# A two-layer hybrid encoder on one core: ten of the first layer's 22 feed-forward blocks by seven products of quarter size, the second layer's state-space maps prepared in the other twelve blocks

## The reference, cut to what matters

```python
for l in range(2):                       # DEPTH
    ...                                  # attention branch, state-space branch, gates, W_o
    x = x + (gate_a * branch_a + gate_b * branch_b) @ w_o[l]
    x = x + _swiglu(_rmsnorm(x, norm2_g[l]), w_ffn_gate[l], w_ffn_up[l], w_ffn_down[l])

def _swiglu(x, w_gate, w_up, w_down):
    return (jax.nn.silu(x @ w_gate) * (x @ w_up)) @ w_down
```

## Time and profile before

| what | value |
|---|---|
| median of 3 runs | 1522.54 us (1522.38 to 1523.39) |
| the profiled execution's own time | 1524.58 us |
| span of its instructions | 1522.4 us |
| TensorE busy | 1486.8 us, 98% |
| VectorE busy | 1099.5 us, 72% |
| ScalarE busy | 670.6 us, 44% |
| GpSimd busy | 462.0 us, 30% |
| first layer's feed-forward, first product to last | 413.4 to 799.7 us |
| second layer's feed-forward begins | 1167.9 us |

### The profile page before, as it was taken

The page is one execution under the profiler, slowest core; times in us unless marked ns, Lnnn a source line. Parts: engine busy times, 40 slices in busy tenths (PEclk is TensorE's granted clock), DMA queues, the critical chain, the costliest instruction groups (busy, mean ns, idle before and its releaser), DMA issues.

```text
span 1522.4 us, 23041 instructions
## 1 busy us (share of the span) xinstructions
PE 1486.8 (98%) x8954; PEld 1221.0 (80%) x8954; DVE 1099.5 (72%) x1469; ACT 670.6 (44%) x1146; POOL 462.0 (30%) x254
## 2 busy tenths in 40 slices
PE   8999998999999999999999999999999999999998
PEld 3555897878878878887888888887787998998997
DVE  5999888768448997568432782586888995896794
ACT  4563258852452222232332413587435652453361
POOL 0000053544444454443544323444542120110010
PEclk9999999999999999999999999999999999999999
DMA  6568720142333244443437642102331333234223
GB/s 248 163 195 294 296 84 1 43 124 83 97 113 97 77 167 158 145 140 112 163 106 276 214 153 89 56 1 70 111 103 65 111 97 126 84 99 137 70 92 116
DMA packets 73499, 189.51 MB, mean 124 GB/s; under 512 B 23600, under 2 KB 32176, under 8 KB 69296
## 3 DMA queue, kind: packets, MB, share of 16 engines
q1 hardware_dynamic: 41952, 145.18, 28.3%
q10 hardware_dynamic: 31440, 42.87, 8.7%
HBM read 155.52 MB, written 32.51 MB: 124 GB/s over the span
## 4 chain that ended last, share of the span: by engine, by line
PE 67%; DVE 17%; DVEq 5%; ACT 4%; issue 3%; DMA 1%; POOLq 1%; POOL 1%; SPq 0%; ACTq 0%
PE ps L2146 20%; PE ps L2148 20%; PE ps L2147 20%; PE ps L2295 2%; DVE wl L1999 2%; DVE work L1382 1%; ACT prob L1148 1%; PE ps L2201 1%; PE ps L2272 1%; DVEq L1562 1%; DVEq L1509 1%; PE ps L2240 1%; DVE wsum L1990 1%; PE ps L2286 1%; PE ps L2459 1%
## 5 line engine op out<-in xcount | busy, mean ns | idle before, releaser
L632 POOL TENSOR_TENSOR wl<-stage,wh 128x1024 fp32r<-128x1024 f32 x138 | 356.7, 2591 | 645.2 <-ACT wh L730 456.2
L730 ACT ACTIVATE wh<-stage 128x1024 fp32r<-128x1024 f32 (+2 forms) x178 | 181.0, 1023 | 221.9 <-PE ps L2148 103.4
L2146 PE MATMUL ps<-XH,wh 128*128 128x256 f32 x616 | 174.8, 284 | 3.7 <-DVE wl L1999 2.8
L2148 PE MATMUL ps<-XH,wl 128*128 128x256 f32 x616 | 173.8, 282 | 0.0
L2147 PE MATMUL ps<-XLr,wh 128*128 128x256 f32 x528 | 148.5, 281 | 0.0
L2146 PE MATMUL ps<-xg2h,wh 128*128 128x512 f32 x352 | 140.3, 399 | 0.0
L2148 PE MATMUL ps<-xg2h,wl 128*128 128x512 f32 x352 | 139.2, 396 | 0.0
L2147 PE MATMUL ps<-xg2l,wh 128*128 128x512 f32 x352 | 139.2, 396 | 0.0
L2146 PEld LDWEIGHTS ps<-XH,wh 128*128 128x128 f32 x616 | 116.8, 190 | 5.2 <-DVE wl L1999 3.2
L2148 PEld LDWEIGHTS ps<-XH,wl 128*128 128x128 f32 x616 | 116.8, 190 | 0.0
L2201 PE MATMUL ps<-X,slabs 128*128 128x512 f32 x224 | 100.7, 604 | 7.2 <-DMA X<-in_xT 5.8
(11 more groups left out here) (346 smaller groups left out, 3748.0 us busy)
## 6 DMA issues: line engine op xcount, KB each, us to landing
stage<-in_stream SPq DMA_DIRECT2D x178, 512.0 KB, 3.4
stage_more<-in_stream SPq DMA_DIRECT2D x34, 512.0 KB, 3.8
CPTR<-ctd_scr ACTq DMA_DIRECT2D x6, 1664.0 KB, 8.2
slabs<-in_stream SPq DMA_DIRECT2D x17, 512.0 KB, 5.5
InT<-in_scr ACTq DMA_DIRECT2D x6, 1024.0 KB, 6.1
ctd_scr<-CPp SPq DMA_DIRECT2D x4, 1152.0 KB, 7.8
ctd_scr<-CPp ACTq DMA_DIRECT2D x4, 1152.0 KB, 6.6
in_scr<-BPI SPq DMA_DIRECT2D x4, 1024.0 KB, 5.0
```

The costliest lines, as they stand in the source:

```text
L632: pool.tensor_tensor(wl[:, s, :], stage[:, (n - RAW) % STAGES, :], wh[:, s, :].bitcast(F32), ALU.subtract).then_inc(wl_ready, 1)
L730: return act.activation(o, i, ACT.Copy, **kw)
L2146: pe.matmul(o, wt[0], x[0], start=start, stop=False, skip_group_check=onto)
L2148: return pe.matmul(o, wt[1], x[0], start=False, stop=stop, skip_group_check=onto)
```

## The change

The first layer's blocks 0 to 9 (five pairs) go by the seven products, as units q = 0 to 9; the second layer's units become q = 10 to 31. The functions of the scheme are now called for both layers, and so the token operands are made during W_o in both, and the statistic too. After the five pairs the first layer makes `xg2h`/`xg2l` anew (its plain operands, 8 copies on ScalarE and 8 subtractions on VectorE), then the down part of the ten blocks, from the plain stream with its two `stage` buffers and GpSimd's remainders, then the twelve plain blocks, then the last down part. `prepare` is called with at = 0 to 7 after the eight outputs of the first down part, 8 to 31 in the twelve blocks (two slots in each: on TensorE after each slab, on VectorE behind each of L1951 and L1959), 32 to 39 after the last outputs. The fourth block's maps have their own tiles (`BPI_late`, `CPp_late`, `work_late`) where the plain operands lay. The second layer's first gate waits for its stores.

```diff
-HALVES = ((0, 11), (11, 11))
-S_HALF = (S_FFN, S_FFN + 3 * 11)
-S_DOWN = (S_FFN + 2 * 11, S_HALF[1] + 2 * 11)
-HB = 11
+FAST_PAIRS = 5
+HEADB, HB = 2 * FAST_PAIRS, FB - 2 * FAST_PAIRS
+S_HEAD = S_FFN
+S_HALF = S_HEAD + HEADB
+S_DOWN = S_HALF + 2 * HB
-PREP_AT = tuple(10 + 5 * b for b in range(BLOCKS))
+TURNS_AT = 9
+PREP_AT = (11, 16, 22, KT + 2 * HB)
-PARTS = ((0, 4), (4, 4), (8, 3))
+PARTS = ((0, FAST_PAIRS), (FAST_PAIRS, 4), (FAST_PAIRS + 4, 4), (FAST_PAIRS + 8, 3))
+OPENS = (0, 2 * FAST_PAIRS)
...
 # SyncE
+            slabs_to_fast(RAW + 4, S_HEAD, 0)
+            for q in range(OPENS[1] - 2):
+                for i in range(2):
+                    freed_by_pair(q, i)
+                    fast_slab(pair_slab(q) + i + 4)
+            for i in range(2):
+                freed_by_pair(OPENS[1] - 1, i)
+                staged_slab(S_HEAD + i)
+            slabs_to_fast(S_HEAD + 2, LAST, 1)
...
 # GpSimd
+                for q in range(OPENS[l], FASTQ if l else OPENS[1]):
+                    s = pair_slot(q, 3)
+                    pool.wait_ge(op_hi[3], q + 1)
+                    pool.tensor_tensor(wl[:, s, 0:QT], ...).then_inc(op_lo[3], 1)
+                if l + 1 < DEPTH:
+                    for n in range(S_HEAD, SLABS):
+                        remainder(SLABS * l + n)
...
 # ScalarE
+            def head_high(i):
+                act.wait_ge(prod_done, DONE[last_of(0), ("P1", "P6", "P7", "P4")[i]])
+                split(0, S_HEAD + i)
...
+                last_high(h, 2)
+                corner(last)
+                last_high(h, 3)
+                finished(last)
...
+                    for m in range(KT):
+                        copy(xg2h[:, m, :], X[:, m, :], scale=...).then_inc(xh_ready, 1)
+                    for n in range(HEADB):
+                        if n:
+                            split(l, S_HEAD + AHEAD + n)
+                        for m in range(KT):
+                            if down_slot(m, HEADB) == n:
+                                prepare(l + 1, m)
+                    for k in range(HB):
+                        for j in range(2):
+                            split(l, S_HALF + AHEAD + 2 * k + j)
+                        at = FAST_PAIRS + k + 1
+                        prepare(l + 1, KT + 2 * k)
+                        act.wait_ge(gn_ready, at)
+                        act.activation(act1[:, k % 2, :], act1[:, k % 2, :], ACT.Silu).then_inc(silu_ready, 1)
+                        act.wait_ge(hid_ready, at)
+                        copy(hidh[:, k, :], hid[:, k % 2, :]).then_inc(hidh_ready, 1)
+                        prepare(l + 1, KT + 2 * k + 1)
...
 # VectorE
+                    for m in range(KT):
...
+                        tt(act1[:, m % 2, :], ps[:, m % 2, :], RS[:], MUL).then_inc(x_part, 1)
+                        dve.drain()
+                        tt(X[:, m, :], X[:, m, :], act1[:, m % 2, :], ADD)
+                        prepare(l + 1, m)
+                    for k in range(HB):
...
+                        tt(act1[:, b, :], ps[:, 4 + 2 * b, :], RS[:], MUL).then_inc(gn_ready, 1)
+                        prepare(l + 1, KT + 2 * k)
+                        dve.wait_ge(slab_done, RING + SLABS * l + S_HALF + 2 * k + 2)
+                        tt(act2[:], ps[:, 5 + 2 * b, :], RS[:], MUL).then_inc(ffn_free, 1)
...
+                        tt(hidl[:, k, :], hid[:, b, :], hidh[:, k, :].bitcast(F32), SUB).then_inc(hidl_ready, 1)
+                        prepare(l + 1, KT + 2 * k + 1)
...
+                    if l and g == 0:
+                        dve.wait_ge(in_stored[(BLOCKS - 1) % 2], 16 * BLOCKS)
+                        dve.wait_ge(cp_stored, 16 * 2 * BLOCKS)
...
 # TensorE
+                fast_pairs(l, l)
...
+                    pe.wait_ge(rms_ready, 3 * l + 3)
+                    head_down(0, range(2))
+                    corner(last_of(0))
+                    head_down(0, range(2, HEADB))
+                    prepare(l + 1, 0)
+                    for m in range(1, KT):
+                        if m >= 2:
+                            pe.wait_ge(x_part, m - 1)
+                        head_down(m, range(HEADB))
+                        prepare(l + 1, m)
+                    for b in range(HB):
+                        for j in range(2):
+                            n = S_HALF + 2 * b + j
+                            ready(n)
+                            pe.wait_ge(ffn_free, b + 1)
...
+                            prepare(l + 1, KT + 2 * b + j)
```

More of the change, by code:

```diff
@@ new lines, in finished, with fast_pairs @@
+            def finished(q):
+                i = q // 2
+                if q % 2 == 0:
+                    act.wait_ge(gn_ready, hid_count(i))
+                    act.activation(act_[:, i % 2], act_[:, i % 2], ACT.Silu).then_inc(silu_ready, 1)
+                else:
+                    act.wait_ge(hid_ready, hid_count(i))
+                    copy(hid_pair(q)[0], up[:, i % 2]).then_inc(hidh_ready, 1)
+            def fast_pairs(l, h):
+                first, last = first_of(h), last_of(h)
+                for q in range(first, last + 1):
+                    high(2, q)
+                    first_copied(q)
+                    if q < last:
+                        high(0, q + 1)
+                    else:
+                        last_high(h, 0)
+                    five(q)
+                    if q > first:
+                        corner(q - 1)
+                    high(3, q)
+                    two(q)
+                    if q == OPENS[l]:
+                        act.wait_ge(stat_ready, 3 * l + 2)
+                        act.activation(rscol[:], ps[:, 0, 0:TT], ACT.Sqrt, bias=eps[:], scale=1.0 / D_MODEL).then_inc(rms_ready, 1)
+                    if q == OPENS[l] + 1:
+                        act.wait_ge(stat_ready, 3 * l + 3)
+                        copy(RS[:], ps[:, 0, :]).then_inc(rms_ready, 1)
+                    if q < last:
+                        high(1, q + 1)
+                    else:
+                        last_high(h, 1)
+                    if q > first:
+                        finished(q - 1)
+                last_high(h, 2)
+                corner(last)
+                last_high(h, 3)
+                finished(last)
@@ L1497, in input_powers @@
                 if part == 0:
-                    if b >= ahead:
+                    if b >= ahead and not late(l, b):
                         dve.wait_ge(in_stored[(b - ahead) % 2], 16 * (2 * l + (b - ahead) // 2 + 1))
@@ L1552, in output_powers @@
                 else:
-                    if b:
+                    if b and not late(l, b):
                         dve.wait_ge(k_ps, BLOCKS * l + b)
@@ new lines, in down_steps @@
+            def down_steps(h, m, ks):
+                count, s = 2 * PARTS[h][1], fast_slot(m)
+                if 0 in ks:
+                    pe.wait_ge(wl_ready, plain(h, m) + 1 - RAW)
+                    if KT * (h - 1) + m >= 2:
+                        pe.wait_ge(down_read, KT * (h - 1) + m - 1)
+                for k in ks:
+                    pe.wait_ge(hidl_ready, hid_count(PARTS[h][0] + k // 2))
+                    last = products(ps[:, m % 2, :], (wh[:, s, k * P:(k + 1) * P], wl[:, s, k * P:(k + 1) * P]),
+                                    (hid1h[:, k, :], hid1l[:, k, :]), k == 0, k == count - 1)
+                return last
@@ new lines, in fast_down @@
+            def fast_down(h):
+                last, count = last_of(h), 2 * PARTS[h][1]
+                if h == 1:
+                    pe.wait_ge(rms_ready, 3 + 3)
+                down_steps(h, 0, range(2))
+                corner(last)
+                down_steps(h, 0, range(2, count - 2))
+                down_steps(h, 1, range(count - 2))
+                for m in range(2):
+                    down_steps(h, m, range(count - 2, count)).then_inc(slab_done, 1)
+                for m in range(2, KT):
+                    down_steps(h, m, range(count)).then_inc(slab_done, 1)
```

974 lines of the change are left out of this document (461 added, 513 removed).

## The result

The kernel after takes 1558.73 us (median of 5 runs, 1557.53 to 1559.94), the kernel before, run beside it, 1523.39 (5 runs, 1522.38 to 1524.49). The ratio is 1.0232, with a 95% interval of 1.0218 to 1.0246: 35.3 us slower, where 27.5 were forecast (1550 against 1522.5). The profiled execution took 1558.73 us, its span is 1556.9.

The account below looks back on a forecast made before the run. TensorE was taken as bound, VectorE nearly as late. -12.6 + 7.9 - 1.0 - 3.2 + 1.3 + 5.3 + 4.0 + 25.4 + 3 = +30 on the 1522.54 median, rounded down: 1550 us, range 1531 to 1564.

Parts of the forecast that it names:

- first down part: waits for tiles' reads: First down part, outputs 1 to 7: TensorE may be only two outputs ahead of VectorE, +4.0 us, 2.2 up to 7.
- last down part: First layer's last down part: VectorE falls behind by up to one output and catches up, 0, at most 2 us.
- Hand-over: Start of first down part: TensorE begins late, +1.3 us, then waits for the last hidden pair's remainder, +5.3, bounds 3 and 7.
- VectorE's load: Twelve blocks: denser prepare slots and meetings with GpSimd remainders make TensorE wait, +25.4 us, bounds 12 and 31.
- Slot 8's 8.4 us: VectorE's price of prepare slot 8, read in the kernel before's windows and counted in the load of blocks 0 to 2.
- VectorE fits: Twelve blocks: GpSimd's remainders fall beside VectorE's PSUM reads and pauses, so no stall there; 1519 us, chance 0.09.
- a lag that grows from 12 to 27 us: Twelve blocks: VectorE's lateness grows from 12 to about 27 us, of which TensorE can stand some 8.
- Two of its own signs: VectorE over 90% busy from first down part to ninth block would show it right; pauses for TensorE in blocks 2 to 8, wrong.
- Clock: Behind new stalls longer than 2.6 us TensorE's clock falls, mostly covered by waits for VectorE: +3 us, 0 to 9.
- the sum of +30: Whole kernel: all terms added, against the profiled execution's 1524.6 us; from the median, rounded down a little, 1550 us.
- Entry: First layer's seven-product start: same price of beginning as in the second layer, +7.9 us, not below 3 nor much above 8.

Follow-up runs that it names:

- The floor: Kernel with spread map work, four of six operations of each second-layer map left out, first-layer plain feed-forward GpSimd remainders cut to 32 columns: 1519.23 us (0.9967).
- the order mended: Kernel after, eight steps of the second down tile before the first tile's two late steps, remainders of xg2 made between tiles: 1558.22 us (1.0227).
- the few map operations: Kernel after with two of six VectorE operations of each second-layer map: 1530.37 us (1.0038); with the changed down-tile order as well, 1529.46 us (1.0035).
- the two runs that take one side of it away: Kernel after with two of six operations of each second-layer map, 1530.37 us; kernel after with the twelve blocks' GpSimd remainders cut to 32 columns, 1525.69 us.
- The run with the load spread: Kernel after with changed down-tile order, transposes in other banks, own buffers for the first map pair, map work in two-operation pieces over slots 8 to 25: 1531.91 us.
- The fill: Kernel after with products that nothing reads put on TensorE ahead of five long waits, 21.4 us in all: 1557.95 us (1.0221).
- the run with the other banks: Kernel after with second halves of the input maps' transposes of blocks 0 to 2 in PSUM banks 0 and 1: 1551.91 us (1.0177).
- the run with everything together: Kernel with spread map work, plus four PSUM banks for first down tiles, up-projection scale moved behind the last down part, later turns and input matrix: 1523.35 us (0.9993).

## Why the prediction was right, and which terms were off

The direction, the stage and the cause are the forecast ones; the shape of VectorE's lateness and the price of the clock are not. 1558.7 lies inside the range of 1531 to 1564. The floor gives the length of each stage without waits, 57.4, 143.5 and 70.2, so that each term can be read as a difference:

| term | forecast | measured |
|---|---|---|
| seven-product part over its 828 products at 0.118 (97.9) | 7.9 + 1.3 | 10.3 |
| first down part: wait for the last pair's remainder | 5.3 | 5.8 |
| first down part: waits for tiles' reads | 4.0 | 1.9 |
| blocks: waits at slots 14 to 16 | 4.3 + 1.1 + 4.6 | 3.7 + 0 + 4.3 |
| blocks: waits at slots 19 to 21, and block 2 | 3.3 + 5.2 + 0.7 | 1.1 + 5.3 |
| blocks: wait at slot 26 | 6.2 | 5.9 |
| last down part | 0 | 0 |
| clock behind the waits (first down part and blocks) | 3 | 12.6 |
| second layer | 0 | 1.1 |

*Hand-over.* Right in place and size: TensorE wanted the remainder at 528.6, 8.3 us after the last P7's end as forecast, and got it at 534.4. But it was in part no price of its own. With the order mended the feed-forward got shorter by 2.9 us (3.3 with the few map operations), not by 7.5 (the wait and the 1.7 us of pace behind it), since part of VectorE's debt stands at the next read. The other wait of this part, for a tile's read, came to 1.9 us, below the 2.2 to 7 allowed.

*VectorE's load.* The forecast 25.4 us of waits in the blocks are 20.3. The cause named, meetings with GpSimd on top of a denser `prepare`, is shown by the two runs that take one side of it away, 28 and 33 us off. VectorE came to the first block 69.7 us after the end of output 0 (537.2 to 606.9), 11.3 behind the ready gate, where 71 to 77 and 12 to 18 were forecast. (The forecast's own terms, 4 + 11.2 + 56 less up to 8, add up to 63 to 71; the trace has 8.5 us of VectorE's waits for TensorE's tiles in the stretch besides. Slot 8's 8.4 us stands in no row above, but the trace of the kernel before bears it out, 527.7 to 536.1.) The rival "VectorE fits" fails in the kernel as it is.

What the forecast had wrong here is the shape, a lag that grows from 12 to 27 us. Two of its own signs speak against it. VectorE was to be over 90% busy up to the ninth block, and is 78% busy (137.6 of 175.6 us from 541.8 to 717.4); and it has pauses for TensorE in blocks 2 to 8 (13.1 us in blocks 6 and 7, counted from 0), which was named as the sign that there is no deficit. The waits are there all the same, since each comes from one bunch of map work: VectorE falls behind within it, catches up while TensorE waits, and then stands still itself. The run with the load spread shows this from the other side: all the work fits, and 26.8 us come back (banks and hand-over included).

*Clock: the step that was off.* The prediction took +3 because "where TensorE waits for VectorE anyway, a slower TensorE is covered". The two stages are longer than floor and waits by 11.1 - 7.7 = 3.4 and 29.5 - 20.3 = 9.2 us, 12.6 in all, the pace lost at the half level. The fill shows the cover to be thin: of 8.4 us of pace given back, 3.4 were covered and 5.0 were not. By that ratio about 7.5 of the 12.6 us are a cost of their own (an estimate), where 3 was taken, and the rest is VectorE's lateness under another name. The waits, booked at 34.7 in all, came to 28.0; waits and clock together were forecast at 37.7 and came to 40.6. With the entry 1.1 and the second layer 1.1 above, the sum of +30 comes within a microsecond of the +34.5 of the trace. **The mis-sized term is the clock.** That the total lies so near is in part luck: waits 6.7 us too high and a clock 9.6 us too low nearly cancel. The other 2.5 us, between the sum's own 1552.5 and 1550, had been taken off for waits in a row that cover each other; nothing in the trace gives them back.

*Entry.* Of the 10.3, 1.1 is the wait before the first down product, for which 1.3 was taken; the other 9.2 stand against the 7.9 that were read in the second layer. The first layer's entry waits 2.6 us for `wl` and has its 3.4 us at half clock, as there; where the further 1.3 lie was not traced.

## What to carry to other kernels

A stage in which TensorE is never idle can still be nearly full on VectorE: before work is taken off TensorE there, VectorE and GpSimd have to be added up over the shorter stage, and an operation of VectorE with two SBUF inputs and one of GpSimd take turns instead of overlapping. The sum alone doesn't settle it: here all the work fitted once it was spread, and as it lay, in bunches and behind shared banks and buffers, it cost 27 us. Work that is made in the gaps of another loop should be cut small and laid evenly, with buffers enough that its stores and copies are no link of the chain: here this, with the banks and the hand-over, brought back 27 of 35 us. A mended wait gives back less than its length while the engine behind it is late: the hand-over's 7.5 us gave 3, and the fill's 8.4 us of pace gave 5. Mend the load first and the order after.

## What the runs showed of the hardware

- In the first feed-forward of the kernel after, the granted clock fell to half at or just behind each of the seven waits of 1.9 to 5.9 us, for 3.4 us (the waits of 1.9, 2.6, 3.7 and 5.8) or 6.8 (those of 4.3, 5.3 and 5.9), and not after the two of 1.1. The wait's length doesn't settle which: the one of 5.8 has 6.8 us behind it in the run with the other banks, and one of 4.4 has 6.8 with the hand-over alone and 3.4 with the few map operations besides; in the kernel before it did not fall after 1.5 and 1.7 us. Products that nothing reads, put into the idle time, kept it at 1.00 around four of the five waits.
- In the second layer, 75 to 105 us after its start, the clock sometimes falls, with the same instructions; the one wait there is 0.8 us in the kernel after, where the clock holds, and 0.8 us too in the runs with the other banks and with the fill, where it falls (1.4 in the run with everything together). The kernel after has 1.00 and the run with everything together 0.83. First the kernel after, then that run, 75 to 105 us after each one's second layer begins:

```profile
908.00:938.00 30.00, 29.16 (x306) 25.16 (x304) 25.50 (x35) 4.82 (x6) 10.07 (x4) 1.00 0.58 199
```

```profile
874.00:904.00 30.00, 28.58 (x269) 25.24 (x268) 21.01 (x26) 4.52 (x6) 9.11 (x4) 0.83 0.49 177
```

Small products (128x64 and 64x64) lie between the large ones there. It fell in the profiled executions of nine of the fourteen kernels, and the second layer is 725 to 730 us long with the drop and 722 to 724 without. So gains of 4 us in the first layer are hard to see in the whole: the run with everything together ends its feed-forward at 799.25 us, where the kernel before does at 799.7, and its profiled execution took 1530.7 us. What decides it stays open; it was not tried.
- In the twelve blocks, with two GpSimd remainders to a block, VectorE's operations of 1.21 to 1.24 us with two SBUF inputs last 1.90 to 2.08 on average and those of 1.35 to 1.39 last 1.35 to 2.81: single ones last as long as alone or up to 3.5, by what they meet, and the worst case of 3.43 is not the rule. Operations that read PSUM and SBUF keep their 0.69 us.
